# The expert loop of an encoder kernel: down one block later, up in contraction halves of 512 columns

## The reference, cut to what matters

```python
def grouped_moe(x, router_w, router_bias, w_gate, w_up, w_down):
    ...
    e_idx, gw = route(x2, router_w, router_bias)
    ...
    order = jnp.argsort(flat_e)
    ...
    padded = (counts + MOE_BLOCK - 1) // MOE_BLOCK * MOE_BLOCK
    ...
    def expert_block(args):
        xb, e = args
        h = jax.nn.silu(xb @ w_gate[e]) * (xb @ w_up[e])
        return h @ w_down[e]

    yp = lax.map(expert_block, (xp.reshape(n_blk, MOE_BLOCK, D), blk_e)).reshape(P, D)
    y_assign = yp[dest] * gw.reshape(A)[order][:, None].astype(yp.dtype)
    y = jax.ops.segment_sum(y_assign, sorted_tok, num_segments=T)
```

## Time and profile before

| | us |
|---|---|
| median of 3 runs | 2327.24 |
| lowest, highest | 2322.62, 2336.02 |
| profiled execution | 2328.09 |
| its span | 2326.4 |
| TensorE busy | 2177.5 (94%) |
| VectorE busy | 1320.5 (57%) |
| ScalarE busy | 992.8 (43%) |
| GpSimd busy | 196.2 (8%) |

### The profile page before, as it was taken

The page is one execution under the profiler, slowest core; times in us unless marked ns, Lnnn a source line. Parts: engine busy times, 40 slices in busy tenths (PEclk is TensorE's granted clock), DMA queues, the critical chain, the costliest instruction groups (busy, mean ns, idle before and its releaser), DMA issues.

```text
span 2326.4 us, 35484 instructions
## 1 busy us (share of the span) xinstructions
PE 2177.5 (94%) x13296; PEld 1830.2 (79%) x13296; DVE 1320.5 (57%) x2102; ACT 992.8 (43%) x1649; POOL 196.2 (8%) x236
## 2 busy tenths in 40 slices
PE   8899988999999899999788999899999989999998
PEld 7778957989889677777687886598988877777774
DVE  2775476533244766666767746835314466666667
ACT  2355565123332255555235547612323224555553
POOL 0000011000000331000200001100000022200004
PEclk9899989999999899999899999899999989999999
DMA  4045111232100599999511112123211038999996
GB/s 156 37 157 192 37 73 56 73 109 73 56 26 35 193 377 374 380 378 363 209 55 37 37 37 92 38 73 104 78 37 55 37 148 322 376 379 375 379 379 237
DMA packets 78548, 385.64 MB, mean 166 GB/s; under 512 B 10472, under 2 KB 11864, under 8 KB 43608
## 3 DMA queue, kind: packets, MB, share of 16 engines
q1 hardware_dynamic: 55264, 327.83, 37.6%
q0 software_dynamic: 10096, 30.38, 3.6%
q10 hardware_dynamic: 13064, 25.75, 3.0%
HBM read 352.79 MB, written 46.07 MB: 171 GB/s over the span
## 4 chain that ended last, share of the span: by engine, by line
PE 77%; DVE 12%; ACT 7%; issue 2%; DMA 1%; DVEq 0%; POOL 0%; ACTq 0%; SPq 0%; POOLq 0%
PE bank L2116 37%; PE bank L2593 10%; PE bank L2567 9%; PE bank L2557 8%; PE bank L2448 2%; DVE weight_slots_parts L1380 2%; PE bank L2132 2%; PE bank L2402 1%; PE bank L2533 1%; ACT x_transposed L1062 1%; PE bank L2285 1%; ACT weight_slots_parts L914 1%; PE bank L2256 1%; ACT scratch L1018 1%; DVE scratch L1532 1%
## 5 line engine op out<-in xcount | busy, mean ns | idle before, releaser
L2116 PE MATMUL bank<-weight_slots_parts,x_transposed_parts 128*128 128x256 f32 x2496 | 466.6, 289 | 4.5 <-ACT mixer_region L965 2.8
L2116 PEld LDWEIGHTS bank<-weight_slots_parts,x_transposed_parts 128*128 128x128 f32 x2496 | 397.0, 196 | 5.5 <-ACT mixer_region L965 3.2
L1824 DVE TENSOR_TENSOR weight_slots_parts<-weight_slots,mixer_region_parts 128x2048 fp32r<-128x2048 f32 x140 | 321.3, 2314 | 85.9 <-ACT mixer_region_parts L1207 85.8
L1207 ACT ACTIVATE mixer_region_parts<-weight_slots 128x2048 fp32r<-128x2048 f32 x140 | 261.0, 1909 | 23.7 <-ACT x_transposed L1282 18.1
L2116 PE MATMUL bank<-x_transposed_parts,weight_slots_parts 128*128 128x512 f32 (+1 forms) x1024 | 266.5, 348 | 1.8 <-DVE mixer_region L1489 1.8
L1380 DVE TENSOR_TENSOR weight_slots_parts<-weight_slots,weight_slots_parts 128x2048 fp32r<-128x2048 f32 x58 | 132.9, 2292 | 223.5 <-ACT weight_slots_parts L914 223.0
L2593 PE MATMUL bank<-weight_slots,x_transposed 128*128 128x512 f32 x560 | 246.4, 593 | 0.0
L2567 PE MATMUL bank<-mixer_region_parts,x_transposed_parts 128*128 128x256 f32 x1120 | 207.3, 283 | 0.4 <-DVE weight_slots_parts L1824 0.4
L2116 PEld LDWEIGHTS bank<-x_transposed_parts,weight_slots_parts 128*128 128x128 f32 x1024 | 183.4, 196 | 24.4 <-DVE mixer_region L1489 3.3
L2557 PE MATMUL bank<-mixer_region_parts,x_transposed_parts 128*128 128x512 f32 x560 | 193.0, 416 | 5.6 <-DVE x_transposed_parts L1829 5.6
L2593 PEld LDWEIGHTS bank<-weight_slots,x_transposed 128*128 128x128 f32 x560 | 103.4, 190 | 117.9 <-issue 101.7
(11 more groups left out here) (311 smaller groups left out, 3565.7 us busy)
## 6 DMA issues: line engine op xcount, KB each, us to landing
weight_slots<-in_w_gate SPq DMA_DIRECT2D x70, 1024.0 KB, 7.3
weight_slots<-in_w_up SPq DMA_DIRECT2D x70, 1024.0 KB, 7.1
weight_slots<-in_w_down SPq DMA_DIRECT2D x70, 1024.0 KB, 7.6
weight_slots<-in_w_in SPq DMA_DIRECT2D x20, 1024.0 KB, 5.0
slots_y<-x_transposed ACTq DMA_DIRECT2D x66, 256.0 KB, 7.2
weight_slots<-in_wkv_mem SPq DMA_DIRECT2D x16, 1024.0 KB, 4.9
slots_y<-in_consts SPq DMA_DIRECT2D x6, 2304.0 KB, 18.1
weight_slots<-in_w_out SPq DMA_DIRECT2D x8, 1024.0 KB, 5.1
```

Of the source, the lines that this page charges most:

```text
L1207: nc.scalar.activation(hi, raw, ACT.Copy).then_inc(moe.high_ready, 1)
L1824: v.tensor_tensor(lo, raw, hi.bitcast(F32), ALU.subtract).then_inc(moe.low_ready, 1)
L2116: ins = pe.matmul(ps, lhs[i](k), rhs[j](k), start=k == 0 and a == 0, stop=k == ks - 1 and a == 2)
```

## The change

The order on all engines but GpSimd is written anew, and the up matrix is laid out as gate is: part 2 holds the first four contraction steps for all 512 columns and part 3 the others. Both sum into bank 3, with 24 products of 512 columns together; the gated product is one instruction of 512 columns. In the loop, block b does gate and up, turns the next block's x, and then computes down of block b-1; only after that it turns its own hidden values. The first block is written out ahead of the loop without a down, the last one after it with two: down of the block before stands between its gate and its up, and its own down comes at the end, with weights that are loaded into gate's places. In the layer after, the first units go into other slots, since down's slot is the first to come free. The code that is cut is marked with dots.

```diff
+SLOT_ORDER = ((0, 1, 2), (1, 0, 2))
 ...
                     def load_up(e, h, signal):
-                        sp.dma_start(expert_part(2 + h)[0], by_k(w_up[l, e, h])).then_inc(signal, 16)
+                        sp.dma_start(expert_part(2 + h)[0], by_k(w_up[l, e][:, 2048 * h:2048 * h + 2048], 4)).then_inc(signal, 16)
 ...
+                    with sp.Fori(1, n_blocks - 1) as b:
+                        e = sp.value_load(r_bei[0:1, bass.ds(b + 1, 1)], min_val=0, max_val=NE - 1)
+                        sp.wait_ge(moe.ga_done, b + 1)
+                        load_gate(e, 0, moe.ga_loaded)
 ...
                         e = sp.value_load(r_bei[0:1, bass.ds(b, 1)], min_val=0, max_val=NE - 1)
 ...
+                        sp.wait_ge(moe.y_filled, 2 * b + 2)
                         load_down(e, 0, moe.dl_loaded)
+                        sp.wait_ge(moe.y_filled, 2 * b + 3)
                         load_down(e, 1, moe.dr_loaded)
+                    e = sp.value_load(r_bei[0:1, bass.ds(n_blocks - 1, 1)], min_val=0, max_val=NE - 1)
+                    sp.wait_ge(moe.ga_done, n_blocks)
+                    load_down(e, 0, moe.ga_loaded, 0)
+                    sp.wait_ge(moe.g_filled, n_blocks + 1)
+                    load_down(e, 1, moe.gb_loaded, 0)
 ...
+                    def expert_block(b, first):
+                        if not first:
+                            copy_hidden(b)
+                        silu(b)
+                        split_part(0, moe.ga_loaded, b + 2)
+                        split_part(1, moe.gb_loaded, b + 2)
+                        act.wait_ge(moe.xT_filled, 2 * b + 4)
+                        block_xT()
+                        split_part(2, moe.ul_loaded, b + 2)
+                        if not first:
+                            store_output(b, yb, 0)
+                        split_part(3, moe.ur_loaded, b + 2)
+                        if not first:
+                            store_output(b, yb, 1)
 ...
+                    b = n_blocks - 1
+                    copy_hidden(b)
+                    silu(b)
+                    store_output(b, yb, 0)
+                    store_output(b, yb, 1)
 ...
+                    copy_hidden(n_blocks)
 ...
+                    def gated(b):
                         dve.wait_ge(moe.g_ready, b + 2)
                         dve.wait_ge(moe.u_filled, b + 2)
+                        v.tensor_tensor(hb[:, :], gact[:, :], banks[3][:, :], ALU.mult).then_inc(moe.h_done, 1)
+
+                    def expert_block(b):
+                        low_part(0, 4 * b + 5)
+                        gated(b)
+                        low_part(1, 4 * b + 6)
+                        low_block_xT(b + 1)
+                        low_part(2, 4 * b + 7)
+                        low_part(3, 4 * b + 8)
 ...
+                    add_stored(0)
+                    add_stored(1)
+                    if l < DEPTH - 1:
+                        low_weights("q0")
+                    for i in range(2, 6):
+                        add_stored(i)
 ...
+                    def three_parts(ps, x_hi_, x_lo_, part, first, last):
+                        _, lo, hi = parts[part]
+                        k0 = 4 * (not first)
+                        for k in range(4):
+                            for a, (x_, w_) in enumerate(((x_hi_, hi), (x_hi_, lo), (x_lo_, hi))):
+                                ins = pe.matmul(ps, x_[:, k0 + k, :], w_[:, k, :],
+                                                start=first and k == 0 and a == 0, stop=last and k == 3 and a == 2)
+                        return ins
+
+                    def up(b, low):
+                        pe.wait_ge(moe.h_done, b + 1)
+                        for h in range(2):
+                            pe.wait_ge(moe.low_ready, low + h)
+                            three_parts(banks[3][:, :], xbT_hi, xbT_lo, 2 + h, h == 0, h == 1).then_inc((moe.ua_done, moe.u_filled)[h], 1)
 ...
+                    gate(0, 4)
+                    up(0, 6)
+                    pe.wait_ge(moe.x_loaded, 16)
+                    turn_block(xb)
+                    turn_hidden(0)
+                    with pe.Fori(1, n_blocks - 1) as b:
+                        gate(b, 4 * b + 4)
+                        up(b, 4 * b + 6)
+                        pe.wait_ge(moe.x_loaded, 16 * b + 16)
+                        turn_block(xb)
+                        down(b)
+                        turn_hidden(b)
 ...
+                    gate(b, 4 * b + 4)
+                    down(b)
+                    up(b, 4 * b + 6)
+                    turn_hidden(b)
+                    down(n_blocks, 0)
```

More of the change, by code:

```diff
@@ L634, in loads_of @@
         def loads_of(name):
-            return 16 * ((now[0] * len(UNITS) + UNIT[name]) // SLOTS + 1)
+            earlier = sum(n % SLOTS == slot_of(name) for n in range(len(UNITS))) if now[0] else 0
+            return 16 * (earlier + UNIT[name] // SLOTS + 1)
         with nc.Block() as block:
@@ L1292, in expert_block, with copy_hidden @@
[L1292 to L1301 removed]
+                    def copy_hidden(blocks):
+                        act.wait_ge(moe.hT_filled, blocks + 1)
+                        nc.scalar.activation(hbT[:, :, :], banks[4][:, :].rearrange("p (k t) -> p k t", k=4),
+                                             ACT.Copy).then_inc(moe.hT_ready, 1)
@@ new lines, in turn_hidden, with down @@
+                    def turn_hidden(b):
+                        pe.wait_ge(moe.h_done, b + 2)
+                        for k in range(4):
+                            ins = pe.transpose(banks[4][:, k * P:(k + 1) * P], hb[:, k * P:(k + 1) * P], ident)
+                        ins.then_inc(moe.hT_filled, 1)
+                    def down(blocks, part=4):
+                        pe.wait_ge(moe.hT_ready, blocks + 1)
+                        for h in range(2):
+                            pe.wait_ge((moe.yl_ready, moe.yr_ready)[h], blocks + 1)
+                            if part:
+                                pe.wait_ge((moe.dl_loaded, moe.dr_loaded)[h], 16 * blocks + 16)
+                            else:
+                                pe.wait_ge((moe.ga_loaded, moe.gb_loaded)[h], 16 * blocks + 16)
+                            for k in range(4):
+                                ins = pe.matmul(banks[5 + h][:, :], hbT[:, k, :], parts[part + h][0][:, k, :], start=k == 0, stop=k == 3)
+                            ins.then_inc(moe.y_filled, 1)
```

220 lines of the change are left out of this document (78 added, 142 removed).

## The result

The changed kernel takes 2350.47 us (median of 5 runs, 2348.17 to 2355.36), the kernel before 2329.61 us in its 5 runs: a ratio of 1.0084 (95% interval 1.0066 to 1.0102), 20.9 us longer. Forecast were 2335 us and a range from 2324 to 2349. So the sign of the shift is right, its size is nearly three times the +7.5 of the sum, and the time lies 1.5 us above the range. The profiled execution spans 2348.9 us against 2326.4.

A forecast was written before the change was run, and what follows sets the result against it. TensorE, never waiting in the steady loop, was taken as the bound. Starts -3.9, loop -5.8, clock +1.8 and ends +15.4 summed to +7.5 us on the profiled 2328.09; forecast 2335, range 2324 to 2349.

The forecast's parts named there:

- The chain behind the load: Loop: from gate's start through load, splits and low parts to the next gate, 11.4 us plus landing; period taken as 19.25.
- the clock: Gate 1 of each layer: TensorE's clock may drop after a 4 us wait; +1.8 for both, bounds 0 and 1.84 per layer.
- the longer ends: Last block of each layer: spread turns to last down's end take 27.32 us instead of 19.59; +7.7 per layer, 15.4.
- the end of layer 1: After layer 1's last block: store, gather and sums hang on the last down's end alone; +7.7 us.
- starts: First blocks: gate 1 starts 2.0 us sooner in layer 0 and 1.9 in layer 1; together -3.9.
- periods: Steady loop blocks: period 19.25 us instead of 19.42 and 19.45, gaining 2.4 and 3.4 us, 5.8 in all.
- end of layer 0: Layer 0's end hangs on early gathers: sixth gather +4.3, last down's end shifting the layer +4.2 too, so counted once.
- The wide up: Up in the loop: 24 products of 512 columns take 5.49 us instead of 5.75 for 48 of 256; gain 0.26 per block.
- DMA takes the loop: Rival, chance 0.20: gate loads land after 7.8 us and their chain sets the loop's period, 19.7 us; +8.2, total 2349.

The follow-up runs named there:

- run 7: Changed kernel with the edits of run 1 and run 2, and unread products (three of 512 columns, one of 256) around the first block's hidden turns: 2328.19 us, 0.9999.
- run 12: Kernel of run 7 with up in column halves of 256 again: 2341.46 us, ratio 1.0058 to the kernel before.
- run 1: Changed kernel with ScalarE's copy of x ahead of splitting gate weights part 1, and VectorE's low part of x ahead of that of part 1: 2333.8 us, 1.0021.
- run 3: Changed kernel with five unread fp32 products of 512 columns around the first block's turns of the hidden part: 2346.5 us, 1.0083.
- run 2: Changed kernel with GpSimd's additions at the end of layer 1 waiting for VectorE's last addition of a gathered row: 2344.75 us, 1.0080.
- run 5: Changed kernel with down of the block before placed ahead of the last gate, not behind it: 2366.87 us, 1.0160.
- run 4: Changed kernel without the load of the second half of the down weights in the loop, the last ones loaded being reused: 2341.41 us, 1.0059.

## Why the prediction was wrong

The chain behind the load, the clock and the longer ends were named rightly, and one step was false: that the end of layer 1 hangs on TensorE's end alone. It cost most, 6.5 us over the forecast. The other groups of the sum were sized too low, all the same way: clock 3.9, starts 2.9, periods 2.4 and end of layer 0 1.7.

- *The wide up, 0.26 us a block.* Right in kind, and too small: 0.35 (runs 7 and 12). I took up at gate's 5.49 us; in one row with gate it adds 5.40 (10.90 in all). The Trainium skill (TensorE: Matmul & The Clock Gate, section "Back-to-back issue gap") would have given 0.06 us; with 13.3 us between runs 7 and 12 the measurement decides against it.
- *The chain behind the gate load.* The sum of 11.4 us + landing is right to 0.2 us: with a landing of 8.51 it gives 19.9, and the block took 20.04. Wrong is how I used it. I put one landing of 7.85 into it and got 0.09 us over TensorE's own period. But a block is late by what its landing has over the threshold, and an early one gives nothing back: over the 28 blocks the loops are 7.5 us longer than in run 1, 0.27 a block. An idle gap in the rows is besides 0.24 us short of what it costs, since a gate without a wait begins 0.24 us ahead of the modelled end of the product before it: the block of 20.04 us has a gap of 0.72 and is 0.96 late. (The 11.17 us that the chain shows for gate and up behind the wait, where it is 10.90 without one, is the same thing: from gate's first product to the first turn it is 11.01 and 10.98.) The loop gained 3.4 us instead of 5.8.
- *The starts.* The same chain with the shortest landings gave 17.8 and 19.3 us from gate 0 to gate 1; measured 18.97 and 21.05. In layer 1 gate 0 itself was slow (the load left 4.6 us behind its start, not 3.2): the granted clock was 0.50 in it from 1933.5 to 1936.8 us, which it was not before, and no run shows whether that comes from the change. In layer 0 ScalarE could begin its split 6.9 us after the issue of the load, not 5.2 (805.58 to 812.45); the split ended at 814.37, and VectorE had other work first:
```profile
815.17 2.29 DVE L1852 TENSOR_TENSOR weight_slots_parts<-weight_slots,mixer_region_parts 128x2048 fp32r<-128x2048 f32 x1 [0.23 <-DVE mixer_region_parts L1406]
```
That x stood behind the second part was in my list of terms, and not among the things that could be late.
- *The clock.* The mechanism was named and its bounds were too narrow. I took 0.9 us and at most 1.84 a layer, from a single gate. There the low clock lay over 9 products, by a window in the kernel before:
```profile
806.10:809.40 3.30, 3.30 (x9) 2.52 (x9) 3.02 (x11) 0.00 (x0) 1.08 (x2) 0.50 0.02 3
```
In gate 1 of the changed kernel it lay over 13 and 14, and cost 2.8 us a layer (run 3).
- *The ends.* TensorE's part is right to 0.2 us (27.5, forecast 27.3). The failed sentence is that "in layer 1 what follows hangs on that end alone". VectorE's last addition, in step with the early gathers, now falls together with GpSimd's: 3.9 us (run 2). Most of what is left of the 6.5 are, in run 2 against the kernel before, the store's landing (6.64 us instead of 5.75) and the first sums (2.07 us instead of 1.12). In layer 0 the early gathers were the right chain (run 5), 1.9 us later than reckoned (21.15 behind the turns, not 19.2), 0.9 of it since their output landed in 6.66 us and not 5.75.
- *The rivals.* "DMA takes the loop" named 2349, which is what came, but not for its reason: its share went to 0.99 in run 1 while the wait vanished. The median came near its number because five terms went the same way, which is luck for that rival.

## What to carry to other kernels

Where a chain with a spread latency feeds a full engine, sum the excess over the slack block by block, not the mean; then look which link of that chain could stand earlier without cost. Here two steps set one place ahead, the copy of x on ScalarE and its low part on VectorE, gave back 15.5 of the 20.9 us by the medians (13.6 of 22.5 by the spans). A share of 0.98 on the queues says that they are in use, not that they are the bound: leave a sixth of the weights out, or shorten the chain, and see. And a software pipeline pays at both ends of every loop: with 16 and 19 blocks in a layer and an engine that was full already, 8 to 9.5 us at each end ate what the wider products and the shorter starts had given.

## What was not expected of the hardware

- VectorE and GpSimd in turn: an addition on VectorE with both inputs in SBUF (1.28 us alone) took 5.77 beside two of GpSimd's of 2.33 us each, also from SBUF, that is, nearly the sum of the three; with one input in a PSUM bank (128x512 each) it kept its time. In all five kernels where the two meet it ends 1.09 to 1.10 us after GpSimd's second addition, also in run 4, where it had a start of 0.56 us:
```profile
2313.21 6.30 DVE L1964 SCALAR_TENSOR_TENSOR x<-mixed,x 128x1024 f32<-128x1024 f32 x1
2313.77 4.65 POOL L863 TENSOR_TENSOR x<-x,scratch 128x1024 f32<-128x1024 f32 x2
```
By the Trainium skill (SBUF — State Buffer, section "Who interferes with whom") an operation of VectorE with two inputs in SBUF contends with one of GpSimd that reads SBUF, since the second input comes through a read interface that both share, and the order of issue decides which of the two blocks. The trace agrees as to which operations suffer. It differs in that VectorE's record begins 0.02 to 0.56 us ahead of GpSimd's, and VectorE waited for both of GpSimd's all the same.
- The queues moved 384 to 385 GB/s over 229 and 306 us (runs 1 and 7), with a median landing of the gate loads of 7.4 us in both (7.3 at 376, in the kernel before).
